# Attention heads of a four-layer decoder on one core: latent scores by pairs of heads in two products, four transposes a head instead of six

## What is computed

```python
def dense_causal_attention(q, k, v, decay=None):      # fox and mla; blocks of 128 queries
    s = jnp.einsum('bqhd,bkhd->bhqk', qi, k) * scale  # (+ decay[t] - decay[s] in fox)
    s = jnp.where(mask, s, NEG)                       # keys <= query
    p = jax.nn.softmax(s, axis=-1)
    return jnp.einsum('bhqk,bkhd->bqhd', p, v)

def mla_mixer(h, w_a, g_q, g_kv, w_uq, w_ukv, w_o, cos, sin):
    cq, ckv, kr = jnp.split(h @ w_a, [384, 640], axis=-1)       # kr: 32 wide, one for all heads
    cq, ckv = rms_norm(cq, g_q), rms_norm(ckv, g_kv)
    q_nope, q_rope = jnp.split((cq @ w_uq).reshape(B, L, 16, 64 + 32), [64], axis=-1)
    q_rope, k_rope = apply_rope(q_rope, cos, sin), apply_rope(kr[:, :, None, :], cos, sin)
    k_nope, v = jnp.split((ckv @ w_ukv).reshape(B, L, 16, 64 + 64), [64], axis=-1)
    qf = concat([q_nope, q_rope]); kf = concat([k_nope, k_rope for every head])   # 96 wide
    return dense_causal_attention(qf, kf, v).reshape(B, L, 1024) @ w_o
```

## Time and profile before

| | |
|---|---|
| time, median of 3 | 1332.93 us (1330.98 to 1333.79) |
| the profiled execution | 1333.88 us, of which 1332.1 are its span |
| TensorE, matmuls | 1296.4 us busy, 97% |
| VectorE | 938.3 us, 70% |
| ScalarE | 793.8 us, 60% |
| GpSimd | 225.8 us, 17% |
| TensorE's granted clock | 0.995 of full speed over the span |
| chain that ended last | TensorE 82%, VectorE 7%, ScalarE 5%, issue 3% |

### The profile page before, as it was taken

One profiled execution on the slowest core, in us unless ns is written; L12 is line 12 of the kernel. 1 busy time (PEld: TensorE's weight loads), 2 busy tenths in 40 slices (PEclk: granted clock), 3 DMA queues, 4 the chain that ended last, 5 costly groups with the idle time before them and its releaser, 6 DMA issues.

```text
span 1332.1 us, 29945 instructions
## 1 busy us (share of the span) xinstructions
PE 1296.4 (97%) x10381; PEld 1252.5 (94%) x10381; DVE 938.3 (70%) x1877; ACT 793.8 (60%) x1625; POOL 225.8 (17%) x208
## 2 busy tenths in 40 slices
PE   7999999999998999999998999999999999999997
PEld 7999999999887999999987899999999899999997
DVE  4765877765787877765678687776567667777665
ACT  4565666654565676664476667666446565766643
POOL 1000044420000034330001003433000000244300
PEclk9999999999999999999998999999999999999999
DMA  7432465556421455556442045555645334465562
GB/s 267 140 110 80 143 189 185 178 180 198 133 91 49 130 185 184 180 155 213 155 127 80 33 143 187 187 172 165 208 139 158 111 112 127 144 187 189 174 218 83
DMA packets 56723, 202.80 MB, mean 152 GB/s; under 512 B 6208, under 2 KB 8256, under 8 KB 56512
## 3 DMA queue, kind: packets, MB, share of 16 engines
q1 hardware_dynamic: 56640, 201.68, 47.4%
HBM read 200.61 MB, written 1.05 MB: 151 GB/s over the span
## 4 chain that ended last, share of the span: by engine, by line
PE 82%; DVE 7%; ACT 5%; issue 3%; DMA 1%; POOL 1%; ACTq 0%; DVEq 0%; POOLq 0%; SPq 0%
PE ps L385 23%; PE ps L389 22%; PE ps L388 22%; PE ps L535 2%; PE ps L553 2%; ACT probs L889 2%; DVE w_lo L1260 1%; PE ps L424 1%; PE ps L518 1%; PE ps L430 1%; PE ps L427 1%; ACT w_hi L839 1%; DMA raw<-in_weights 1%; POOL gated L1234 1%; DVE scores L1320 1%
## 5 line engine op out<-in xcount | busy, mean ns | idle before, releaser
L1260 DVE TENSOR_TENSOR w_lo<-raw,w_hi 128x1024 fp32r<-128x1024 f32 x377 | 461.1, 1225 | 230.3 <-ACT w_hi L839 228.9
L385 PE MATMUL ps<-h_hi,w_hi 128*128 128x272 f32 (+1 forms) x1752 | 508.6, 290 | 1.8 <-DVE q_rope L1526 1.0
L389 PE MATMUL ps<-h_hi,w_lo 128*128 128x272 f32 (+1 forms) x1752 | 505.8, 289 | 0.0
L388 PE MATMUL ps<-h_lo,w_hi 128*128 128x272 f32 (+1 forms) x1752 | 499.6, 285 | 0.0
L839 ACT ACTIVATE w_hi<-raw 128x1024 fp32r<-128x1024 f32 x377 | 395.0, 1050 | 147.7 <-PE ps L385 136.9
L385 PEld LDWEIGHTS ps<-h_hi,w_hi 128*128 128x128 f32 x1752 | 329.1, 188 | 8.4 <-issue 5.4
L388 PEld LDWEIGHTS ps<-h_lo,w_hi 128*128 128x128 f32 x1752 | 330.0, 188 | 0.3
L389 PEld LDWEIGHTS ps<-h_hi,w_lo 128*128 128x128 f32 x1752 | 328.9, 188 | 0.0
L385 PE MATMUL ps<-hid_hi,w_hi 128*128 128x272 f32 (+2 forms) x636 | 185.4, 292 | 2.2 <-DVE w_lo L1260 1.9
L388 PE MATMUL ps<-hid_lo,w_hi 128*128 128x272 f32 (+2 forms) x636 | 183.1, 288 | 0.0
L389 PE MATMUL ps<-hid_hi,w_lo 128*128 128x272 f32 (+2 forms) x636 | 183.0, 288 | 0.0
(11 more groups left out here) (184 smaller groups left out, 1727.3 us busy)
## 6 DMA issues: line engine op xcount, KB each, us to landing
raw<-in_weights SPq DMA_DIRECT2D x377, 512.0 KB, 3.7
cst<-in_consts SPq DMA_DIRECT2D x1, 1795.5 KB, 12.1
h<-in_x SPq DMA_DIRECT2D x2, 544.0 KB, 5.8
out<-h SPq DMA_DIRECT2D x8, 128.0 KB, 1.7
```

What stands on the lines that cost most here:

```text
L385: m = pe.matmul(b, whi, xhi, start=n == 0, stop=False)
L388: pe.matmul(b, whi, xlo, start=False, stop=False)
L389: m = pe.matmul(b, wlo, xhi, start=False, stop=n == len(tiles) - 1)
L1260: return dve.tensor_tensor(out_, a_, b_, op)
```

## The change

Scores and probabilities get one layout, with the middle chunk first (columns 0 to 143), then the 16 meta queries (144 to 159), then the last chunk (160 to 431). The last chunk has its keys in the order 256 to 271, then 0 to 255, in keys, scores, masks, decays and probabilities. With that, four transposes of 128x128 a head cover all (`TURNED`); their 16-key corners come to lie in rows 0 to 47 of the third, and are copied by two small instructions. The third product of `mix` takes the corners of all three chunks, 48 columns in three groups of 16; for it, rows 0 to 31 of the third value tile are filled by two DMAs a layer, issued by ScalarE (`corner_values`), and `mix` waits for them once a layer.

In mla two heads share a tile of queries and of keys, as in fox, and a score is two products that are added in PSUM: one over 64 rows, one over 32 rows with the rotary part. The 32-wide rotary key is in the weights four times, so that the rotated key comes out for four row groups at once, and GpSimd's copies are gone. `rope_r` writes once instead of four times. `kv_rstd` is made from the reciprocals that exist per token, by three small products. The first query and key panels move ahead of the last rotary one. `take_k` moves ahead of both `normalise` in mla, and ahead of the second split in fox; in swa masks and rotation move ahead of `out_lo`, and the split ahead of `normalise`. The table load moves behind the splits of the second panel of down.

```diff
-SCOL = (0, 16, 160, 432)
-PCOL = (0, P, 3 * P)
+SCOL = ((P + TAIL, P + 2 * TAIL), (0, P + TAIL), (P + 2 * TAIL, P + 2 * TAIL + T))
+KCOL = ((TAIL, 2 * TAIL), (TAIL, P + 2 * TAIL), (0, T))
+TURNED = (0, P + 3 * TAIL, 2 * P + 3 * TAIL, P)
+PT1, PT2, PTW = T, T + P, T + P + 3 * TAIL
-    sizes = [QT] * (ROPE_PANELS - 2) + [QT, KT] * PAIRS
+    sizes = [QT, QT, KT, QT] + [QT, KT] * (PAIRS - 1)
...
-            def score(a, kind, hn):
...
+            def score_latent(a, m):
+                if m:
+                    pe.wait_ge(masked, HEADS * a + 2 * m)
                 for ch, (lo, hi) in enumerate(CHUNKS):
+                    hi_q = max(hi, P)
+                    for s in range(2):
+                        r = slice(HD * s, HD * s + HD)
+                        pe.matmul(ps[0:hi_q - lo, 2 + s, slice(*SCOL[ch])], queries[r, m, lo:hi_q],
+                                  keys[r, m, slice(*KCOL[ch])], start=True, stop=False)
+                    for s in range(2):
+                        t = MLA_ROPE * ((2 * m + s) % 4)
+                        r = slice(t, t + MLA_ROPE)
+                        ins = pe.matmul(ps[0:hi_q - lo, 2 + s, slice(*SCOL[ch])],
+                                        queries[r, PAIRS + m // 2, lo:hi_q], keys[r, PAIRS, slice(*KCOL[ch])],
+                                        start=False, stop=True)
+                ins.then_inc(scored, 2)
...
-                one(PT1 + TAIL - P, 1, P)
-                one(PTW - P, 2, 2 * P, TAIL)
-                one(0, 0, 0)
-                one(N_META, 1, 0)
-                one(N_META + P, 2, 0)
-                one(PT1 + TAIL, 2, P).then_inc(transposed, 1)
+                for n, col in enumerate(TURNED):
+                    t = pe.transpose(b[:, n * P:(n + 1) * P], pr[:, col:col + P], ident)
+                t.then_inc(transposed, 1)
...
+                        if t < 2:
+                            dst, src = o[:, (0, N_META + P)[t]:T], pt[:, (0, PT1)[t]:(PT1, PT2)[t]]
+                        else:
+                            dst = o[:, 0:3 * P].rearrange("p (g c) -> p g c", g=3)[:, :, 0:TAIL]
+                            src = pt[:, PT2:PTW].rearrange("p (g c) -> p g c", g=3)
...
+            def corner_values(cols):
+                for n, chunk in enumerate((1, 0)):
+                    act.dma_start(v_tok[TAIL * n:TAIL * n + TAIL, 2, 0:cols],
+                                  v_tok[0:TAIL, chunk, 0:cols]).then_inc(v_corners, 16)
...
-                if n % 2:
-                    act.preload_act_table_set(TABLES)
+                    if k == 1 and n % 2:
+                        act.preload_act_table_set(TABLES)
...
-                        for t in range(4):
-                            r = slice(32 * t, 32 * t + 32)
-                            ins = tt(queries[64:96, 4 * m + t, :], y[r, 0, :], y[r, 1, :], ALU.add)
-                        ins.then_inc(roped, 1)
+                        tt(queries[:, PAIRS + m, :], y[:, 0, :], y[:, 1, :], ALU.add).then_inc(roped, 1)
...
-                        tt(keys[0:64, 2 * m, :], b[0:64], kv_rstd[0:64], ALU.mult)
-                        tt(keys[0:64, 2 * m + 1, :], b[64:128], kv_rstd[64:128], ALU.mult).then_inc(bank_free, 2)
+                        tt(keys[:, m, 0:TAIL], b[:, 2 * P:T], kv_rstd[:, 2 * P:T], ALU.mult)
+                        tt(keys[:, m, TAIL:T], b[:, 0:2 * P], kv_rstd[:, 0:2 * P], ALU.mult).then_inc(bank_free, 2)
...
-                    own.link(dve.reciprocal(kv_rstd, kv_rstd))
```

More of the change, by code:

```diff
@@ L517, in score_pair @@
                         r = HD * s
-                        ins = pe.matmul(ps[0:hi_q - lo, 2 + s, SCOL[ch]:SCOL[ch + 1]],
-                                        queries[r:r + HD, m, lo:hi_q], keys[r:r + HD, m if fox else m // 4, 0:hi],
+                        ins = pe.matmul(ps[0:hi_q - lo, 2 + s, slice(*SCOL[ch])], queries[r:r + HD, m, lo:hi_q],
+                                        keys[r:r + HD, m if fox else m // 4, slice(*KCOL[ch])],
                                         start=not fox, stop=not fox or ch == 2)
@@ L728, in sum_squares @@
                             pe.wait_ge(lat_sq, k + 1)
-                            if not is_q:
-                                pe.matmul(ps[:, 6, 0:T], ones, y[:, k % 4, :], start=k == ks[0], stop=k == ks[-1])
                         cols = ((0, P), (N_META, N_META + P), (N_META + P, T)) if is_q else \
@@ L783, in _ @@
                     swap(gated[:])
+                    pe.wait_ge(lat_scale, 1)
+                    for n, (lo, hi) in enumerate(((0, P), (P, 2 * P), (2 * P, T))):
+                        ins = pe.matmul(ps[:, 6, lo:hi], lat_col[0:hi - lo, 1, n:n + 1].broadcast_to([hi - lo, P]),
+                                        ident[0:hi - lo, 0:hi - lo], start=True, stop=True)
+                    ins.then_inc(lat_spread, 1)
                     for n in range(6):
@@ L787, in _ @@
                             swap_rope(n // 4)
-                    for r in range(2):
-                        panel(sq, uq, pq, 0, r, from_latent(0), None, 0)
-                    for m in range(PAIRS + 1):
+                    for j, first in ((0, 0), (1, 0), (2, QT)):
+                        panel(sq, uq, pq, 0, j, from_latent(first), None, 0)
+                    pe.wait_ge(q_taken, 1)
+                    panel(sq, uq, pq, 0, 3, from_latent(0), None, 0, pq + 1)
+                    for m in range(1, PAIRS + 1):
                         p = pq + 2 + 2 * m
@@ L1455, in decay_rows @@
                             own.link(copy(pick[:], c("pick")))
-                        row = scores[0:16, 0, :]
-                        total = row[:, SCOL[2]:SCOL[3]]
+                        both = scores[0:16].rearrange("p s c -> p (s c)")
+                        row, keys0 = both[:, 0:SW], SCOL[2][0] + TAIL
+                        total = both[:, keys0:keys0 + T]
                         own.link(dve.tensor_tensor_scan(total, zero, lnu, 0.0, ALU.mult, ALU.add))
-                        copy(row[:, SCOL[0]:SCOL[1]], total[:, 0:CHUNKS[0][1]])
-                        own.link(copy(row[:, SCOL[1]:SCOL[2]], total[:, 0:CHUNKS[1][1]]))
+                        copy(row[:, slice(*SCOL[0])], total[:, 0:CHUNKS[0][1]])
+                        copy(row[:, SCOL[2][0]:keys0], total[:, 2 * P:T])
+                        own.link(copy(row[:, slice(*SCOL[1])], total[:, 0:CHUNKS[1][1]]))
                         copy(dec[HD:HD + 16], row)
@@ L1498, in take_k @@
                         b = bank(pq + 2 * m + 1, 2)
-                        copy(keys[:, m, :], b).then_inc(bank_free, 2)
+                        copy(keys[:, m, 0:TAIL], b[:, 2 * P:T])
+                        copy(keys[:, m, TAIL:T], b[:, 0:2 * P]).then_inc(bank_free, 2)
                     for m in range(PAIRS + 1):
@@ L1558, in _ @@
                             rope_q(m - 1)
+                        if m >= 4:
+                            out_lo(a, m - 4)
+                        if m < PAIRS:
+                            split_units(a, "q", 0, m)
                         if m >= 2:
```

176 lines of the change are left out of this document (83 added, 93 removed).

## The result

The kernel after takes 1337.45 us (median of 7 runs, 1335.88 to 1341.59), the kernel before 1333.57 on the same chip (7 runs, 1330.98 to 1335.41). The ratio is 1.0037 (95% interval 1.0028 to 1.0046). The forecast of 1314 and its range, 1305 to 1325, both missed, and the sign with them.

A forecast was written before the change was run, and what follows sets the result against it. TensorE, busy 97%, was taken as the bound, with VectorE near it in swa. Terms: fox -7.1, swa -4.2, mla -5.0, last down stage -3.0, DMAs and swa tails +0.5, sum -18.8, giving 1314 us, range 1305 to 1325.

The forecast's parts named there:

- The step that failed: Swa: the split ahead of both `normalise` covers a 0.80 us wait; period 7.76 to 7.0, 4.2 us saved.
- The bound I gave: Swa's saving: from nothing, if a wait appears between the masks and `normalise`, to 5.5 us.
- The clock: Half-speed falls behind TensorE's waits in mla and the last down stage go with those waits: about 1.7 us each.
- ScalarE's copies in swa: Swa: copies grow 0.16 us a head, second exponentials come 0.3 later, still inside the split's cover.
- (a): Rival: freed time turns into waits; swa stays at 7.76, mla gains 1 instead of 5; 1322 us; 20%.
- (b): Rival, mla scores: 32-row products not side by side, changes dearer; +19 us, 1329; 5%, and 5% for half (1324).
- Fox: Both fox layers, TensorE-bound: 16 pairs at 0.41 us less, plus 0.5 from earlier `take_k`; 7.1 us saved.
- Mla, the scores: Latent scores: two heads side by side, 0.16 us a change of shape; a pair 2.16 to 2.6, +4 us.
- Mla, the waits: Mla: third pair's scores 2.6 us earlier, 0.8 before the first scores, 1.2 of idle in steady pairs; mla overall -5.
- The last down stage: Table load moved back: 1.3 us of the 1.91 wait go, plus 1.7 of slow clock; -3.0 us.

The follow-up runs named there:

- a1: Kernel after with swa's split on VectorE put back behind both `normalise`: 1324.41 us, ratio to before 0.9941.
- a8: Kernel after with ScalarE making `w_hi` right behind the first head's exponentials in swa, VectorE's order untouched: 1325.11 us, ratio to before 0.9943.
- b5: Kernel before with only the new VectorE order in swa, old layouts and copies kept: 1342.39 us, ratio to before 1.0073.
- a4: a1 plus ScalarE copying the turned probabilities ahead of both heads' exponentials in swa: 1319.93 us, ratio to before 0.9905.
- b11: Kernel before with ScalarE copying the turned probabilities ahead of both heads' exponentials in swa: 1327.62 us, ratio to before 0.9962.
- a3: Kernel after with VectorE's whole order in swa as before: 1328.91 us, ratio to before 0.9968.
- a6: a4 plus the middle chunk's 32-row products first in the latent scores, for fewer changes of row height: 1315.03 us, ratio to before 0.9880.
- b9: Kernel before with only the down stages' table load at its new, later place: 1331.74 us, ratio to before 0.9985.
- a7: a4 with the table load back at the head of the down stages: 1320.39 us, ratio to before 0.9905.

## Why the prediction was wrong, step by step

- **The step that failed** is swa: "The new order lays the split, 1.2 us, ahead of both `normalise`, which covers the wait of 0.80". It took the split for free work of VectorE. The split has an input, `w_hi`, and ScalarE makes it behind both heads' exponentials, so it can't cover a wait for the second of these: its own wait ends later. The kernel before shows it already, on ScalarE and on VectorE:
```profile
398.74 1.04 ACT L839 ACTIVATE w_hi<-raw 128x1024 fp32r<-128x1024 f32 x1
```
```profile
399.89 1.21 DVE L1260 TENSOR_TENSOR w_lo<-raw,w_hi 128x1024 fp32r<-128x1024 f32 x1
```
`w_hi` was done at 399.78, 0.1 us ahead of the split in its old place; ahead of the `normalise` of 398.87 it couldn't have started. In place of the wait of 0.80 came one of 3.03. Forecast -4.2, measured +14.2; shown by a1 (one place, 13 us), a8 (the input earlier, 12 us) and b5 (the order alone, +9.7 us by the ratio). The bound I gave, "nothing, if a wait appears between the masks and `normalise`", named the place and left out the price: I never added up the loop that such a wait closes.
- **The clock.** TensorE's waits of 1.2 to 2.6 us in each turn were followed by falls to half speed in five turns of six, mean 0.87 over 60 us of swa. I weighed the clock only where a wait went, not where one might come. In the steady turns of swa that cost nothing, as the turns of 9.99 us at either clock show. Where I did weigh it, in mla, I took the fall as gone with the wait: it came in five of the seven traces with after's mla, all with waits of 0.4 us and less ahead of the scores. That after's own trace had none is luck.
- **ScalarE's copies in swa**: "still inside that cover". They took 1.52 for 0.92 a pair (+0.6, not +0.3), on the loop in every order but those with the copies first (a4, b11). It is the whole of a3's 8.39 for 7.77.
- **The likeliest of the rivals, (a)**, had swa stay at 7.76. Freed time did turn into waits, but past the point where it started. None of my rivals had swa lose time, and 0.03 for slower rested on (b) in full, the wrong mechanism.
- **Fox**: right. -3.8 and -3.6 for 7.1. TensorE binds there, and four transposes fewer a pair are time won: 0.45 a pair in mla's rows, where 0.44 was forecast.
- **Mla, the scores**: right in mechanism (two heads side by side, a price on each change of height), size off. The term was +0.5 a pair, from 2.16 to 2.6; measured from the same point to the same point it is +0.96, or 7.7 us over eight pairs for the 4 forecast. I had read the length of a merged row as the time that the scores hold TensorE. A change between heights is 0.15 (a6), as I had it at 0.16. What was too small is, by subtraction, the two ends, from `mix` and back to the panels: 2.86 - 1.46 - 5 x 0.15 = 0.65 for the 0.32 I gave; no run takes the ends alone. The Trainium skill, TensorEngine Tiling (Array Packing), section Key Properties, says that a change of tiling mode drains the engine. By that rule the order by turns is the worst, and a6 agrees: 0.31 us back for two changes fewer.
- **Mla, the waits**: the third pair's scores came 722.20 - 710.58 = 11.6 us behind the first, as forecast (about 12). But the steady pairs run at 6.72 us where they ran at 6.4 to 6.7: TensorE is now the bound, so the 1.2 I took for their idle went into the longer scores. -2.1 for -5.0 in this trace, -0.9 by the means.
- **The last down stage**: right on the wait (0.53 left, 0.6 forecast), half right on the sum. Of the -3.0, 1.7 was the clock's fall behind the old wait. In five traces with the load at its old place it came in two; b5 and b11 had the same wait (1.92 and 1.88) and no fall. -2.5 in the table, 1.5 by the means, 2.0 by b9's ratio.

With swa's split in its old place, a1 lies 8.3 us under before (1332.69 in those runs), where the forecast without its -4.2 for swa would have been 14.6 under. Of the 6.3 missing, swa accounts for 2.1 (104.3 for 102.2) and mla for 2.8 (2.2 in a1's trace, for 5.0); the other 1.4 is not assigned.

## What to carry to other kernels

Before you move an operation into a wait as its cover, ask when its own inputs come, on the other engine's queue, in that same turn. Then write the whole loop out across the engines, each step behind what it needs, and add it up: when the sum is above every engine's busy time, the order is the bound, and the cheapest gain may be a third engine's order (here ScalarE's copies, 5 us in either kernel). An in-order engine behind a late input turns a cover into a gate.

## What the runs showed of the hardware

- Float32 products over 32 rows of two heads run side by side like those over 64 (0.73 us for four of 272 columns in either), and each change between the two heights costs TensorE about 0.15 us.
- Small ScalarE copies cost by their number more than by their size: those of 32x32 and 16x16 take 170 and 175 ns, that of 128x384 takes 481, and a head's three together 0.76 us of the loop. A short duration needn't be a short hold: before, the next copy began 0.07 us after the start of the 16x16 one, now 0.17 to 0.20 after a small one. The groups by line (busy us, mean ns, idle before):
```profile
L916 ACT ACTIVATE probs_t<-ps 128x384 f32<-128x384 f32 x64 | 30.8, 481 | 6.2 <-PE ps L540 2.8 <-PE ps L559 2.6
L919 ACT ACTIVATE probs_t<-ps 16x16 f32<-16x16 f32 x64 | 11.2, 175 | 0.7
L917 ACT ACTIVATE probs_t<-ps 32x32 f32<-32x32 f32 x64 | 10.9, 170 | 0.0
```
- The clock's fall to half isn't tied to one wait. In after's swa it came in five turns of six; the turn without one had the shortest wait, 1.19 us against 1.28 to 2.60, but in b5's swa a wait of 2.32 had no fall and waits of 1.96 had one. Behind a wait of 1.9 at the head of the last down stage it came in before and in a7, and not in b5 and b11. In a4 it came once on the first latent scores, for 6.8 us, where a1, with the same code in that stage, had none. So one trace's fall, or its absence, is no basis for a term.
- What a fall costs goes by who binds: nothing in a turn of after's swa, which VectorE and ScalarE set, and 1.4 us on one pair of latent scores, for which TensorE alone was at work (4.30 for 2.86, a4).
